# A single-core transformer kernel: Fourier mixer with the token transform applied to h itself, router logits from transposes of h, and the Fourier stage's two ends taken by token halves

## What is computed

```
h_l = rms_norm(x, norm1_g) * (1 + sc1) + sh1
hg = h_l.reshape(B, L, 8, 128)
f = fft.fftn(hg, axes=(1, 3), norm='ortho').real      # over 256 tokens and within groups of 128 columns
x = x + g1 * (f.reshape(B, L, D) @ fnet_w_o + fnet_b_o)
h2 = rms_norm(x, norm2_g) * (1 + sc2) + sh2
logits = h2 @ router;  top 2, softmax over the two
x = x + g2 * sum over the two experts of gate * (silu(h2 @ w1) * (h2 @ w3)) @ w2
return rms_norm(x, final_g)
```

## Time and profile before

| what | us |
|---|---|
| median of 3 runs | 2924.43 (2920.01 to 2926.23) |
| the profiled execution's own time | 2927.81 |
| its span in the profile | 2926.0 |
| TensorE busy | 2735.4 (93%) |
| VectorE busy | 2089.1 (71%) |
| ScalarE busy | 1680.5 (57%) |
| DMA moved | 664.54 MB, mean 227 GB/s |

### The profile page before, as it was taken

The page is one execution under the profiler, slowest core; times in us unless marked ns, Lnnn a source line. Parts: engine busy times, 40 slices in busy tenths (PEclk is TensorE's granted clock), DMA queues, the critical chain, the costliest instruction groups (busy, mean ns, idle before and its releaser), DMA issues.

```text
span 2926.0 us, 35565 instructions
## 1 busy us (share of the span) xinstructions
PE 2735.4 (93%) x12809; PEld 2231.0 (76%) x12809; DVE 2089.1 (71%) x2477; ACT 1680.5 (57%) x2177; POOL 88.9 (3%) x111
## 2 busy tenths in 40 slices
PE   7999899999999999889679997699999999999997
PEld 6888778878877778777458886587878878787885
DVE  4556658777567655542567773699988989998897
ACT  4456454454477654432444442377787777778775
POOL 2000000000000000022000000000000000000000
PEclk9999999999999999989889998799999999999999
DMA  8545137678453355421048861299999999999994
GB/s 287 188 158 180 45 123 261 234 260 289 159 171 124 103 193 188 157 101 58 0 151 303 305 244 64 76 353 338 353 347 334 359 333 352 339 351 344 343 350 166
DMA packets 278012, 664.54 MB, mean 227 GB/s; under 512 B 12869, under 2 KB 21345, under 8 KB 277905
## 3 DMA queue, kind: packets, MB, share of 16 engines
q1 hardware_dynamic: 263344, 609.74, 58.8%
q0 software_dynamic: 14560, 53.36, 5.2%
HBM read 662.00 MB, written 1.05 MB: 227 GB/s over the span
## 4 chain that ended last, share of the span: by engine, by line
PE 82%; DVE 11%; ACT 4%; issue 2%; DMA 0%; DVEq 0%; ACTq 0%; SPq 0%
PE ps L2243 24%; PE ps L2245 24%; PE ps L2244 24%; DVE w_lo L1412 3%; ACT w_hi L733 2%; PE ps L2359 1%; PE ps L2431 1%; PE ps L2932 1%; PE ps L2847 1%; DVE xt L2115 1%; DVE small L2002 1%; PE ps L2639 0%; DVE xn L1497 0%; PE ps L2891 0%; PE ps L2859 0%
## 5 line engine op out<-in xcount | busy, mean ns | idle before, releaser
L1412 DVE TENSOR_TENSOR w_lo<-w_raw,w_hi 128x1024 fp32r<-128x1024 f32 x1156 | 1386.9, 1222 | 464.6 <-ACT w_hi L733 437.8
L733 ACT ACTIVATE w_hi<-w_raw 128x1024 fp32r<-128x1024 f32 x1156 | 1210.7, 1057 | 824.6 <-PE ps L2245 823.7
L2243 PE MATMUL ps<-w_hi,act_hi 128*128 128x512 f32 (+1 forms) x3424 | 1348.5, 394 | 48.3 <-DVE w_lo L1412 31.6
L2245 PE MATMUL ps<-w_lo,act_hi 128*128 128x512 f32 (+1 forms) x3424 | 1324.1, 387 | 0.0
L2244 PE MATMUL ps<-w_hi,act_lo 128*128 128x512 f32 (+1 forms) x3424 | 1322.7, 386 | 0.0
L2243 PEld LDWEIGHTS ps<-w_hi,act_hi 128*128 128x128 f32 x3424 | 648.5, 189 | 194.6 <-DVE w_lo L1412 49.8
L2245 PEld LDWEIGHTS ps<-w_lo,act_hi 128*128 128x128 f32 x3424 | 647.7, 189 | 132.2
L2244 PEld LDWEIGHTS ps<-w_hi,act_lo 128*128 128x128 f32 x3424 | 649.2, 190 | 125.3 <-issue 2.9
L1403 DVE SCALAR_TENSOR_TENSOR scr<-scr,small 128x1024 f32<-128x1024 f32 x98 | 125.3, 1279 | 0.0
L864 ACT ACTIVATE act_hi<-ps 128x512 fp32r<-128x512 f32 (+1 forms) x87 | 62.7, 721 | 78.9 <-PE ps L2359 78.9
L1543 DVE TENSOR_TENSOR act_lo<-ps,act_hi 128x512 fp32r<-128x512 f32 (+1 forms) x87 | 74.1, 852 | 35.4 <-ACT act_hi L864 35.4
(11 more groups left out here) (452 smaller groups left out, 1553.8 us busy)
## 6 DMA issues: line engine op xcount, KB each, us to landing
w_raw<-in_moe_w SPq DMA_DIRECT2D x336, 1024.0 KB, 6.1
scr<-in_ada_w POOLq DMA_DIRECT2D x48, 1024.0 KB, 6.6
w_raw<-in_ffn_w_gate SPq DMA_DIRECT2D x44, 1024.0 KB, 5.2
w_raw<-in_ffn_w_up SPq DMA_DIRECT2D x44, 1024.0 KB, 5.4
w_raw<-in_ffn_w_down SPq DMA_DIRECT2D x44, 1024.0 KB, 4.9
w_raw<-in_ff_w SPq DMA_DIRECT2D x42, 1024.0 KB, 5.8
w_raw<-in_odd_w_in SPq DMA_DIRECT2D x20, 1024.0 KB, 5.1
w_raw<-in_even_w_in SPq DMA_DIRECT2D x14, 1024.0 KB, 5.1
```

The costliest lines, as they stand in the source:

```text
L733: act.activation(w_hi[:, g % SPLITS, 0:c * width], w_raw[:, s % RING, o:o + c * width], ACT.Copy).then_inc(hi_done, 1)
L1412: dve.tensor_tensor(w_lo[:, g % SPLITS, 0:c * width], w_raw[:, s % RING, o:o + c * width], w_hi[:, g % SPLITS, 0:c * width].bitcast(F32), ...
L2243: pe.matmul(out_ap, hi, whi, start=start, stop=False)
L2245: return pe.matmul(out_ap, hi, wlo, start=False, stop=stop)
```

## The change

- `fourier`: the row-wise norm is folded into the token transform's table: `f_w = f_l * rstd` per token block, and TensorE multiplies h itself by it (16 matmuls of 256 columns: cosines of frequencies 0 to 128 and sines of 1 to 127, the other half following by symmetry). The result is scaled by A1 on ScalarE, B1 is added at frequency zero, and the group transform makes all 256 columns from them, reading the mirrored frequencies backwards (32 matmuls of 127 to 129 columns). There are no transposes, and no bias matmuls: the bias row times G1 is added to h on VectorE beside the output product, from a row that POOL broadcasts by DMA.
- The dense block ends with `tail`. G2's row is broadcast in its step 0 (`row=True`) and the addition to h is made by token halves (`add_half`, `half_root`, `half_rstd`). `fnet_w_o` also ends with `tail`, into banks 4 to 7.
- Router: h is transposed without the norm (block 0 inside the tail), multiplied by `r_wa = r_w * A2`, and the logits are `rstd * that + r_b`. The gather waits for the places alone. Two granules of the first expert are split before the gather.
- Expert loop: `hi_ahead(2)` and `lo_ahead(2)` before the branch, the first `up` waits for each half of the gathered activations (`ready`), and SP loads one slot more after the last block.
- Some semaphores are merged (`eps_set`, `more_t`, `more_c`, `dl_in`).

```diff
@@ dense block
-            gated(FF2, sums=1, windows=SUMS_DENSE)
-            row_diag(modv[:, MOD_G2:MOD_G2 + 8])
-            mod_columns(1)
-            add_branch()
-            fourier()
-            row_diag(modv[:, MOD_G1:MOD_G1 + 8])
-            add_branch()
+            row_diag(modv[:, MOD_G2:MOD_G2 + 8], rowd)
+            gated(FF2, sums=1, windows=SUMS_DENSE, row=True)
+            fourier()
@@ gated, PE
+                    if row and i == 1:
+                        pe.wait_ge(row_read, n(row_read))
...
+                    if row and i == 0:
+                        pe.wait_ge(silu_done, n.last(silu_done) + 1)
+                        row_broadcast(rowd, 4)
@@ DVE
+            def add_half(tb, bank, half=None):
+                cols = slice(0, DM) if half is None else slice(BANK * half, BANK * half + BANK)
+                link(dve.tensor_tensor(xn[:, tb, cols], banks(bank + 2 * tb, 2)[:, cols], wbc[:, cols], ALU.mult))
+                return dve.tensor_tensor(h[:, tb, cols], h[:, tb, cols], xn[:, tb, cols], ALU.add)
@@ fourier, DVE
+                def table(tb):
+                    link(half_rstd(tb))
+                    dve.tensor_scalar(f_w[:, tb, :], f_l[:, tb, :], rstd[:, tb:tb + 1], None, ALU.mult).then_inc(ft_w, 1)
+                dve.wait_ge(br_done, BR_DENSE)
+                add_half(0, 0).then_inc(h_first, 1)
+                row_diag(modv[:, MOD_G1:MOD_G1 + 8], rowd)
+                lo(1)
+                dve.wait_ge(tab_in, 64)
+                table(0)
+                dve.tensor_scalar(f_b16, modv[:, MOD_B1:MOD_B1 + 8], 16.0, None, ALU.mult)
+                lo(1)
+                dve.wait_ge(gran_used, end)
+                add_half(1, 0).then_inc(h_ready, 1)
+                lo(1)
+                dve.tensor_tensor(r_wa, r_w, bc(modv[:, MOD_A2:MOD_A2 + 8], 8), ALU.mult)
+                dve.tensor_tensor(r_wb, r_w, bc(modv[:, MOD_B2:MOD_B2 + 8], 8), ALU.mult)
+                table(1)
+                lo(1)
+                row_taken(0)
...
+                dve.wait_ge(ctx_in, 48)
+                link(dve.tensor_tensor(fnb, fnb, wbc[:], ALU.mult))
+                lo(1)
+                for tb in range(TB):
+                    ins = dve.tensor_tensor(h[:, tb, :], h[:, tb, :], fnb, ALU.add)
...
+                row_diag(modv[:, MOD_G2:MOD_G2 + 8])
+                dve.memset(mo_acc, 0.0)
+                dve.memset(mo_PT, 0.0).then_inc(mo_ptc, 1)
+                lo(1)
@@ fourier, PE
+                for tb in range(TB):
+                    pe.wait_ge(ft_w, tb + 1)
+                    if tb:
+                        row_broadcast(rowd, 0)
+                    for c in range(DC):
+                        ins = pe.matmul(ps[:, 4 + c // 2, (c % 2) * TOKENS:(c % 2 + 1) * TOKENS], h[:, tb, c * P:(c + 1) * P], f_w[:, tb, :],
+                                        start=tb == 0 and c % 2 == 0, stop=tb == TB - 1 and c % 2 == 1)
...
+                pe.wait_ge(row_read, n(row_read))
                 for g in range(8):
...
+                    pe.matmul(out_g[:, 0:P + 1], f_g[:, 0, :], z[:, 0:P + 1], start=g % 2 == 0, stop=False)
+                    pe.matmul(out_g[:, P + 1:TOKENS], f_g[:, 0, :], z[:, P - 1:0:-1], start=False, stop=False)
+                    pe.matmul(out_g[:, 1:P], f_g[:, 1, :], z[:, P + 1:TOKENS], start=False, stop=False)
+                    ins = pe.matmul(out_g[:, P + 1:TOKENS], f_g[:, 2, :], z[:, TOKENS - 1:P:-1], start=False, stop=g % 2 == 1)
...
+                down(range(4), True, bank=4, ready=ft_lo)
+                pe.wait_ge(ft_lo, n(ft_lo, 2))
+                pe.matmul(ps[:, 2, 0:64], ones, r_wb.rearrange("p c e -> p (c e)"), start=True, stop=True)
...
+                tail(range(4, 8), bank=4, beside=turn)
@@ experts, PE
+                pe.wait_ge(ro_act, 1)
+                logits(0, 0)
+                logits(0, 1)
+                for k in range(2):
+                    pe.wait_ge(*((h_ready, 3) if k else (h_first, 4)))
+                    for c in range(4):
+                        at = (4 * k + c) * P
+                        ins = pe.transpose(ps[:, 2 + k, c * P:(c + 1) * P], h[:, 1, at:at + P], ident)
+                    ins.then_inc(ro_pe, 1)
+                for k in range(2):
+                    pe.wait_ge(ro_dve, k + 2)
+                    ins = logits(1, k)
                 ins.then_inc(mo_lg, 1)
+                row_broadcast(sg, 2)
...
-                    pe.wait_ge(mo_p, n(mo_p))
+                    pe.wait_ge(mo_link, n(mo_link))
...
-                    pe.wait_ge(mo_xl, n(mo_xl, 2))
-                    gated(FF2, 1, beside)
+                    gated(FF2, 1, beside, ready=mo_xl)
@@ experts, DVE
+                add_half(0, 4).then_inc(h_first, 1)
+                link(dve.tensor_reduce(r_b, ps[:, 2, 0:64].rearrange("p (c e) -> p e c", c=DC), AX_X, ALU.add))
+                lo_ahead(2)
+                dve.wait_ge(gran_used, end)
+                add_half(1, 4, 0).then_inc(h_first, 1)
+                add_half(1, 4, 1).then_inc(h_ready, 1)
...
                     gated(FF2, 1, beside)
+                    lo_ahead(2)
@@ experts, ACT
                     gated(FF2, 1, beside)
+                    hi_ahead(2)
@@ SP, after the loop
+            n.block = n_blocks
+            load(moe_from)
```

More of the change, by code:

```diff
@@ L2158, in experts @@
                                            -float(P), None, ALU.add))
+                extra(0)
+                for k in range(2):
+                    gather_half(k)
+                    dve.wait_ge(mo_xc, n.last(mo_xc) + k + 1)
+                    gathered_low(k)
+                    extra(1 + k)
                 dve.wait_ge(mo_ids, 1)
@@ L2257, in up @@
                             pe.wait_ge(alo_done, alo_before + chunk // 2 + 1)
+                        if ready is not None and chunk % 4 == 0:
+                            pe.wait_ge(ready, n(ready))
                         for base, cols, bank in outs:
@@ L2292, in lead, with down @@
                 gp[0] += 4
-            def down(chunks, first=False, final=False, tbs=TB, alo=False):
+            def down(chunks, first=False, final=False, tbs=TB, alo=False, bank=0, ready=None):
                 for i, chunk in enumerate(chunks):
@@ L2306, in down, with tail @@
                 gp[0] += len(chunks)
-            def tail(chunks, free=None, act_low=None):
+            def tail(chunks, free=None, act_low=None, bank=0, beside=None):
                 for tb in range(TB):
@@ L2323, in tail @@
                             h_transposes(0, k - 2, free if k == 3 else 6)
+                        if tb and beside is not None:
+                            beside(k)
                 gp[0] += 4
@@ L2346, in norm, with gated @@
                     pe.wait_ge(alo_done, n.last(alo_done))
-            def gated(ff, tbs=TB, beside=None, scaled=False, closing=None, sums=None, windows=None):
+            def gated(ff, tbs=TB, beside=None, scaled=False, closing=None, sums=None, windows=None, row=False, ready=None):
                 s = steps(ff)
@@ L2391, in gated @@
                 hidden(last)
[L2392 removed]
+                if tbs == TB:
                     if closing:
```

309 lines of the change are left out of this document (162 added, 147 removed).

## The result

The changed kernel takes **2873.9 us** in the median of 4 runs (2871.9 to 2875.2), the kernel before 2925.3 beside it (4 runs, 2920.0 to 2928.5): ratio **0.9825, 95% interval 0.9808 to 0.9842**, 51.4 us less. The profiled execution took 2871.89 us with a span of 2870.1; the one of before was 2.5 us above its own median, so the two spans differ by more than the medians, 55.9 us. By that pair of profiles I sort the time; the stages add up to the 55.9, where the forecast's add up to 52.5. The gather that ends a row is taken where the chain of waits places it (1960.46 before, 1907.70 after).

The account below looks back on a forecast made before the run. Bound by two latency chains of engines waiting for each other, plus eight expert blocks as a TensorE stream. Gains 29.3-0.8+23.1+3.0 = 54.6, less 2.1 for handoffs, gave 52.5 and a forecast of 2872 us, range 2861 to 2887.

Parts of the forecast that it names:

- Fourier (a): Dense block's step 0: moving G2's broadcast and row copy there costs 0.7 us, ends 0 and 3.1.
- Fourier (b) to (d): Fourier stage: token halves cost 0.1 us; token transform, block 1's wait and group transform end at 18.6 us.
- Fourier (e), the clock: Fourier stage: half clock after an idle TensorE hole of 2.6 us costs 1.0 us, ends 0 and 12.5.
- Output product: Product with fnet_w_o: eight transposes and one matmul add 1.2 us, clock gives back 0.4; 0.8 us longer.
- Router (a) and (c): Router: last logit 5.8 us after the output product (a), plus 2.0 us for half clock (c).
- (b): Router: last logit to gather takes 6.4 us, 6.7 before, as the gather waits for the places alone.
- (d): Router: gather to third expert granule takes 15.1 us, of which 1.5 is for the clock.
- Loop: Expert loop: two granules split before the branch save 0.45 us at each of seven boundaries, 3 us in all.
- handoff sum of 2.1: Whole change: some 20 new handoffs of about 0.1 us each cost 2.1 us, bound 0 to 4.
- the clock through both chains (2888): Rival, Fourier stage and router: TensorE's clock stays at 1.2 GHz, 16 us more, 2888 us; chance 0.12.
- The table reload in the loop (2885): Rival, expert loop: reload holds ScalarE, third granule 1.28 us late in each of eight blocks, 2885 us; chance 0.05.

Follow-up runs that it names:

- e8: Changed kernel with four repairs of VectorE's order (dense step 0, Fourier stage, loop entry, gathered columns out at step 4's end): 2858.7 us, ratio 0.9771.
- e1: Changed kernel with both ends taken whole instead of by token halves, block 0's transposes after the tail: 2882.7 us, ratio 0.9857.
- e3: Changed kernel with each of the token transform's 16 matmuls issued twice: 2873.2 us, ratio 0.9829.
- e2: Changed kernel with the expert loop as before: no granules split ahead, both gathered halves awaited, no extra weight slot: 2876.6 us, ratio 0.9844.
- e6: Changed kernel with router logits taken from transposes of the normalized xn again, not of h: 2872.7 us, ratio 0.9818.
- e7: Kernel before the change, with TensorE's holes filled by 128-column products whose result nobody reads: 2915.6 us, ratio to before 0.9962.

## Why the prediction came out

The sum was right (2872 for 2873.9), and mostly for the reasons given. That it was off by 1.9 us only is luck: between the two profiles the sum was 3.4 short (55.9 for 52.5), and that the profiled execution of before lay 2.5 above its median and the one after 2.0 below outweighed it. By terms:

- **Fourier (a), the term that was mis-sized.** I charged 0.7 us for G2's broadcast in step 0 and it cost 1.82: the first product of step 1 came at 1545.85, before at 1544.03. VectorE's timeline of the changed kernel:

```profile
1541.57 1.22 DVE L1603 TENSOR_TENSOR hp<-sg,ps 128x1024 f32<-128x1024 f32 x1 [8.63 <-PE ps L2325]
1543.22 1.23 DVE L1637 COPY wbc<-ps 128x1024 f32<-128x1024 f32 x1 [0.42 <-PE ps L2497]
1544.48 1.22 DVE L1447 TENSOR_TENSOR w_lo<-w_raw,w_hi 128x1024 fp32r<-128x1024 f32 x1
```

  The copy itself ended 0.4 us after the transposes. I had asked when it ends and whether TensorE's transposes cover it, and not what is queued behind it: the next weight split is, and TensorE waited 1.79 us for that. e8 put one split ahead of the copy, and 1.3 us came back. The measured value lay inside my ends (0 and 3.1).
- **Fourier (b) to (d)**: 18.7 forecast, 18.0 measured, with token halves worth 5.9 in that stage (e1), the half columns of the token transform 4.7 (e3), and reversed reads free, as I took them. The rest of the 31.7 no run undoes; it is read from the instructions that are gone: the transposes, the bias products with 5.40 us and the 2.65 of waiting ahead of them.
- **Fourier (e), the clock**: 1.0 charged, 0 in the profile of the change, 1.7 in others. The mean of six profiles is 2 x 1.7 / 6 = 0.6.
- **Output product**: +0.8 forecast, +1.3 measured. The fourth split was in time: no gap of TensorE over 0.4 us stands in the tail.
- **Router (a) and (c)**: last logit 7.1 us after the output product, for 5.8 + 2.0. (The terms that I named for (a), 1.4, 1.35, 0.5, 0.7 and 1.1, add up to 5.1; 5.8 counts the copy twice.) **(b)** 6.0 for 6.4. **(d)** 13.5 for 15.1: VectorE's queue came as built (13.6 forecast to the end of the third granule's split, 13.4 measured), and the 1.5 of clock did not add to it, since TensorE waited for that split anyway.
- **Loop**: 127.20 for a forecast of 127.2; 0.43 of it undone by e2.
- **Not in the sum**: +1.6 us of half clock in the first expert products after the third granule. My handoff sum of 2.1 covered it by luck, not by reason.

Of the rivals, the clock through both chains (2888) did not come: the Fourier stage had 1.00. Half clock did come in the router. I had written against this rival that no stretch of the trace of before shows it for bursts as long as these; that was a misreading, since the gather of before took 6.41 us where 3.57 is its full pace, and in e1 the first eight products of the token transform took 6.39 for 3.72. The table reload in the loop (2885) is refuted by ScalarE's timeline at a block's start,

```profile
2081.70 2.00 ACT L745 ACTIVATE w_hi<-w_raw 128x1024 fp32r<-128x1024 f32 x2
2083.72 1.28 ACT L745 ACT_TABLE_LOAD   x1
2085.01 2.01 ACT L745 ACTIVATE w_hi<-w_raw 128x1024 fp32r<-128x1024 f32 x2
```

where the next split follows the load's end by 0.01 us, as before. The Trainium skill (ScalarE: Activation LUTs, What ACT_TABLE_LOAD costs) adds a drain of about 1.38 us; no run of this case shows it: behind a load that nothing else holds up the next instruction comes within 0.02 us, and ahead of one the longest idle time is 0.37. The Trainium skill (TensorE: Matmul & The Clock Gate, Part 1: The HAM clock gate) says that the point at which the clock changes varies from run to run; the traces agree, with 17.9 or 19.6 us for one and the same stage and 1.95 to 3.59 for block 1's logits.

What stays open: what causes the 5 us of scatter ahead of the dense block; how the router's 25.8 us divide beyond the pieces that e1, e2 and e6 undid, which overlap in part; and what sets the point in the router at which the clock falls (the profiles differ there with and without edits ahead of it).

## What to carry to other kernels

When an instruction that waits is moved onto an in-order engine, price what is queued behind it, not only the instruction: here a copy that ended only 0.4 us behind TensorE's own work cost 1.8 us through the weight split behind it. A wait that shrinks is not yet time gained: in e8 it shrank by 3.3 us, and the work behind it came 1.0 us earlier by the edit. Where one engine feeds another with 10% to spare, side work doesn't get cheaper by standing one or two feeds later; it belongs where the feeder is already idle, and the profile's idle-before column names that place. And when run-to-run scatter is as large as the effect, compare the same stage in two traces from one anchor instruction to the next: e3 and e6 would have been read as "no effect" by their medians alone.

## What the runs showed that I had not expected

- Work that nobody reads made the kernel before 7 to 15 us faster (e7), through the granted clock alone.
- The clock after the same hole of 1.97 us stayed at 1.00 in four profiles and fell in two; in the router, block 1's eight logit products took anything from 3.59 to 1.95 us in different profiles (2.96, 2.58 and 2.12 between), as it fell before, among or behind them.
- The same kernel in two profiles reached the same product 5 us apart (1500.5 and 1495.5), with every stage behind it equal to 0.1 us.
- A negative step on the moving operand of a float32 product cost nothing measurable (0.22 us from start to start with 127 or 129 columns, forwards or backwards).
